# Constants and modulation columns inside the norm stage, output inputs in halves, and a last norm taken block by block

## The chip, the cores and the metric

The kernel runs as one program on 1 core of one Trainium2 chip. Its time is the device time in microseconds (us) of one execution; the time before is 3041.14 us, the median of 3 runs that lie between 3032.96 and 3041.2. TensorE multiplies matrices, VectorE and ScalarE work elementwise, GpSimd splits some of the weights, and SyncE issues most transfers (DMAs). In the profile these are PE (with PEld, its weight loads), DVE, ACT, POOL and SP; SPq and ACTq are transfers issued by SyncE and ScalarE.

## The reference

Two blocks over 1024 tokens of width 1024, one after the other, all in fp32. The change touches the seams of the second block:

```python
x = first_block(x, ...)                       # attention + state-space block, ends in rms_norm
mod   = silu(c) @ ada_w + ada_b               # 6 x 1024: shift, scale, gate of two norms
mod_c = silu(c_ctx) @ ada_w + ada_b
pc = modulate(rmsnorm(ctx, norm1_g), csh1, csc1) @ w_in     # 256 context tokens
px = modulate(rmsnorm(x, norm1_g), sh1, sc1) @ w_in         # 1024 tokens
# modulate(h, shift, scale) = h * (1 + scale) + shift
a_x = rwkv_out(rwkv_bidir(...)); b_x = short_conv(px_cv, conv_w)
x = x + g1 * (concatenate([a_x, b_x]) @ w_out)
hx = modulate(rmsnorm(x, norm2_g), sh2, sc2)
x = x + g2 * expert_choice_ffn(hx, router_w, w_gate, w_up, w_down)   # 16 experts
return rmsnorm(x, final_g)
# rmsnorm(x, g) = x * rsqrt(mean(x * x) + 1e-6) * g
```

## The kernel before, in words

The program is a sequence of stages. Each stage is a `Phase`, which holds its SBUF and PSUM tiles and semaphores; when it ends, the semaphores are cleared and a barrier over all engines follows (L85 to L90). Inside a stage every engine has an instruction stream of its own, written out by hand, and they meet only in semaphores. Tokens are taken in blocks of 128 (`P`), rows in `KD` = 8 parts of 128 columns. There is no planner: the order of everything is the order in the code.

**Constants of the second block** (`second_mixer`, L2637). A stage `const2` loads 24 tensors one after the other on SyncE's queue (`load_constants`, L103) and waits for all: two matrices of squares, an identity, twelve level masks of 32 KB, four triangular masks of 64 KB, the norm gain as columns (`n1`), three small tables for the projections, and last two rows of 2048 numbers, shift and scale for tokens and context (`rows`). Then a stage of its own (`affine_columns`, L1440) turns these rows into columns by 16 transposes on TensorE; VectorE adds 1 to the scale and multiplies by the gain: `ab`.

**Norm stage** (`mixer_norms`, L1462). Ten blocks: two of the context, eight of the first block's result `xmid`. SyncE loads into four buffers; from block 4 on each load waits until the block four before it is scaled (L1483). ScalarE squares with a running sum, VectorE makes the mean, ScalarE the root, VectorE the inverse, and scales the rows into `xn`. TensorE turns them by 8 transposes into PSUM; VectorE (columns 0 to 3) and ScalarE (4 to 7) apply `ab`. ScalarE rounds the result to its high part, VectorE subtracts for the low part. In each engine's stream block b's square or mean stands before block b-1's affine part.

**Projections, state recurrence, output.** The tables `mu`, `cls` and `taps` are used in `mixer_projections`, the masks and identity later. The last stage of the mixer is `out_norm` (L1106), named `o2` here; the first block ends in the same function under the name `on`, with other arguments (`late` empty, a norm in the end). For `o2` the left factor comes from memory in two parts of 2 MB, `aT` and `bT`, each [128, 4, 1024]; they are `late`, and SyncE asks for them first (L1131), then for the eight weight rows of 512 KB, into four buffers, so that weight 4 waits until weight 0 is split (L1134 to L1137). ScalarE and VectorE wait for both parts in full (L1175, L1206), split block 0 of the left factor (`put(0)`), then the weights, then block 1. TensorE does three matmuls for each weight row and half, eight blocks in all, and VectorE multiplies by the gate and adds `xmid`.

**Router and experts** follow, then `final_norm` (L3090): SyncE loads eight blocks and then the gain row, broadcast to all partitions; ScalarE squares all eight; one mean, one root, one inverse for all of them at once; then VectorE multiplies block by block into two buffers, each of which waits from block 2 on for the store of the block two before it (L3135).

Of the kernel before, what the change touches and what calls it, by code (L numbers as in the profile page):

```python
# [1105 lines left out]
def out_norm(nc, name, parts, late, w_dram, split, x_dram, gate, gain, y_dram):  # L1106
# [4 lines left out]
    with Phase(nc, name) as ph:  # L1111
# [9 lines left out]
        names = ("late", "row_loaded", "w_hi", "w_lo", "s_hi", "s_lo", "summed", "gated", "added", "squared", "meaned", "rooted", "inverted",  # L1121
# [6 lines left out]
        with nc.Block() as block:  # L1128
            @block.sync
            def _(sp):  # L1130
                for dst, src in late:  # L1131
                    sp.dma_start(dst, src).then_inc(q["late"], 16)
                for k in range(KD):
                    if k >= 4:  # L1134

                        sp.wait_ge(q["w_lo"], k - 3)
# [28 lines left out]
            def _(act):  # L1165
                def put(b):
                    if b >= 2:

                        act.wait_ge(q["summed"], b - 1)
# [5 lines left out]
                if late:  # L1175
                    act.wait_ge(q["late"], 16 * len(late))
# [20 lines left out]
            def _(dve):  # L1197
# [8 lines left out]
                if late:  # L1206
                    dve.wait_ge(q["late"], 16 * len(late))
# [232 lines left out]
def affine_columns(nc, T, rows, n1, ab):  # L1440

    with Phase(nc, "aff") as ph:
        pc = ph.ps("pc", [P, 2 * KD, 2])
        turned, made, scaled = ph.sem("turned"), ph.sem("made"), ph.sem("scaled")
        with nc.Block() as block:
            @block.tensor
            def _(pe):
                for k in range(2 * KD):
                    last = nc.tensor.transpose(pc[:, k, :], rows[:, k * P:(k + 1) * P], T.ident[0:2, 0:2])
                last.then_inc(turned, 1)  # L1450

            @block.vector
            def _(dve):
                dve.wait_ge(turned, 1)
                for row in range(2):
                    nc.vector.tensor_scalar(ab[:, 2 * row, :], pc[:, KD:, row], 1.0, None, ALU.add).then_inc(made, 1)
                    nc.vector.tensor_copy(ab[:, 2 * row + 1, :], pc[:, :KD, row]).then_inc(made, 1)
                    dve.wait_ge(made, 2 * row + 2)
                    nc.vector.tensor_tensor(ab[:, 2 * row, :], ab[:, 2 * row, :], n1, ALU.mult).then_inc(scaled, 1)


def mixer_norms(nc, T, blocks, parts):  # L1462
# [4 lines left out]
    with Phase(nc, "n2") as ph:  # L1467
# [3 lines left out]
        st = ph.sb("st", [P, 4, N])  # L1471
# [5 lines left out]
        with nc.Block() as block:  # L1477
            @block.sync
            def _(sp):
                for b in range(N):  # L1480
                    if b >= 4:

                        sp.wait_ge(q["normed"], b - 3)  # L1483
# [1802 lines left out]
```

## Time and profile before

| | us |
|---|---|
| median of 3 runs | 3041.14 |
| lowest, highest | 3032.96, 3041.2 |
| profiled execution | 3047.39 |
| its span, first to last instruction | 3045.5 |
| TensorE busy in it | 2514.2 (83%) |
| VectorE busy | 1639.6 (54%) |
| ScalarE busy | 987.2 (32%) |
| GpSimd busy | 631.3 (21%) |

The profile is of one execution. Times in its rows count from the start of the span. A row of the timeline gives the start, the duration, the engine, the line of the kernel, the operation with its output and inputs, how often it is merged into this row, and in brackets how long the engine stood idle before it and what released it. TensorE's granted clock has two levels, 1.2 and 2.4 GHz; the profile gives it as a share of the higher one. Tile names are the program's with digits left out: `b_aT` is `aT`, `n_xt` the norm stage's input buffer, `fin_y` the output buffer of the last norm.

### The profile page before, as it was taken

Reading aid. Unit: us, or ns where it says so; the run is one execution under the profiler, and the core shown is the slowest. Engines: PE = TensorE matmul, PEld = TensorE weight load, DVE = VectorE, ACT = ScalarE, POOL = GpSimd, SP = SyncE. Lnnn points to the kernel's source line nnn. Section 1 sums busy time; section 2 is a strip of 40 time slices with the busy share of each in tenths; the row PEclk is TensorE's granted clock in tenths of the full one; section 3 lists DMA queues with packets and bytes.
Section 4 is the critical chain, followed back from the end, with each engine's and each line's share of the span. In section 5 each row is a group of like instructions: output and inputs, shape, how many; then the busy total and the mean of one; then the engine's idle time right before and its main releaser. Section 6 shows DMA issues by size and latency. Waiting matters only on the chain. (4 is left out here: it accounts for less than half of the span.)

```text
span 3045.5 us, 57305 instructions
## 1 busy us (share of the span) xinstructions
PE 2514.2 (83%) x23846; PEld 1934.9 (64%) x23846; DVE 1639.6 (54%) x2057; ACT 987.2 (32%) x1546; POOL 631.3 (21%) x618
## 2 busy tenths in 40 slices
PE   4698997869989379997857888888763799999993
PEld 1586654546757368886336667774553788888882
DVE  2793447521114322565545556552336499999993
ACT  2111442210013320001324333332211087777772
POOL 0221357212210023220045444430000010110000
PEclk8899999989999679998569999995875599999996
DMA  9232004321113211110231011101533099999993
GB/s 381 70 135 79 10 1 133 100 96 52 34 56 124 94 49 63 49 42 18 102 93 31 18 25 30 26 4 56 190 119 138 20 391 403 398 388 398 399 380 132
DMA packets 132726, 405.60 MB, mean 133 GB/s; under 512 B 55090, under 2 KB 64946, under 8 KB 102690
## 3 DMA queue, kind: packets, MB, share of 16 engines
q1 hardware_dynamic: 119268, 359.53, 31.6%
q0 software_dynamic: 4608, 16.78, 2.3%
q10 hardware_dynamic: 8640, 26.19, 2.2%
q8 instruction: 169, 2.77, 0.4%
q14 instruction: 41, 0.34, 0.0%
HBM read 346.85 MB, written 55.61 MB: 132 GB/s over the span
## 5 line engine op out<-in xcount | busy, mean ns | idle before, releaser
L3039 DVE TENSOR_TENSOR ex_wl<-ew_raw,ex_wh 128x2048 fp32r<-128x2048 f32 x192 | 435.8, 2290 | 42.6 <-ACT ex_wh L3001 39.0
L3001 ACT ACTIVATE ex_wh<-ew_raw 128x2048 fp32r<-128x2048 f32 x192 | 367.6, 1919 | 216.8 <-PEq L89 109.3
L125 PE MATMUL sp_acc<-b2h_hi,sp_wh 128*128 128x512 f32 (+1 forms) x528 | 194.8, 369 | 11.7 <-POOL sp_wl L1614 11.7
L125 PE MATMUL sp_acc<-b2h_lo,sp_wh 128*128 128x512 f32 (+1 forms) x528 | 194.5, 368 | 0.0
L125 PE MATMUL sp_acc<-b2h_hi,sp_wl 128*128 128x512 f32 (+1 forms) x528 | 194.3, 368 | 0.0
L2162 ACT ACTIVATE rc_xt<-rc_ps 128x256 f32<-128x256 f32 x200 | 67.7, 389 | 197.2 <-PE rc_ps L2331 196.6
L2922 POOL DMA_INDIRECT x<-ex_o,ex_at x16 | 26.5, 1656 | 493.1 <-DVE ex_o L3062 493.1
L1100 DVE TENSOR_TENSOR merge_sg<-b_pj,merge_sg 128x512 f32<-128x512 f32 x16 | 11.1, 693 | 218.0 <-ACT merge_sg L1086 218.0
L2229 DVE TENSOR_TENSOR rc_x<-rc_x,rc_ps 128x256 f32<-128x256 f32 x160 | 60.2, 418 | 120.4 <-PE rc_ps L2317 120.1
L125 PE MATMUL merge_acc<-merge_hh,merge_wh 128*128 128x512 f32 x256 | 101.5, 396 | 26.4 <-POOL merge_wl L119 21.1
L125 PEld LDWEIGHTS sp_acc<-b2h_hi,sp_wh 128*128 128x128 f32 x528 | 100.1, 190 | 28.7 <-POOL sp_wl L1614 12.1
L1612 POOL CAST sp_wh<-sp_w 128x1024 fp32r<-128x1024 f32 x26 | 27.1, 1042 | 434.5 <-DMA sp_w<-in_w_conv 250.9
L2910 POOL DMA_INDIRECT ex_xs<-h,ex_at x16 | 26.7, 1667 | 422.1 <-DVE ex_at L3064 398.1
L125 PEld LDWEIGHTS sp_acc<-b2h_lo,sp_wh 128*128 128x128 f32 x528 | 100.2, 190 | 16.5
L125 PEld LDWEIGHTS sp_acc<-b2h_hi,sp_wl 128*128 128x128 f32 x528 | 100.0, 189 | 16.5
L125 PE MATMUL pr_acc<-h_hi,pr_wh 128*128 128x512 f32 x224 | 89.7, 400 | 21.8 <-POOL pr_wl L205 20.1
L2223 DVE TENSOR_TENSOR rc_t<-rc_ps,b_level 128x256 f32<-128x256 f32 x200 | 75.5, 419 | 52.7 <-PE rc_ps L2317 52.3
L2943 PE MATMUL ex_G<-ex_wh,ex_xh 128*128 128x512 f32 x256 | 102.3, 399 | 1.4 <-DVE ex_xl L3044 1.4
L2943 PE MATMUL ex_O<-ex_wh,ex_hh 128*128 128x512 f32 x256 | 100.4, 392 | 1.6 <-DVE ex_hl L3055 1.6
L2943 PE MATMUL ex_U<-ex_wh,ex_xh 128*128 128x512 f32 x256 | 101.1, 395 | 0.0
L2944 PE MATMUL ex_G<-ex_wl,ex_xh 128*128 128x512 f32 x256 | 100.8, 394 | 0.0
L2945 PE MATMUL ex_G<-ex_wh,ex_xl 128*128 128x512 f32 x256 | 100.7, 393 | 0.0
(465 smaller groups left out, 6364.6 us busy)
## 6 DMA issues: line engine op xcount, KB each, us to landing
ew_raw<-in_exp_gate SPq DMA_DIRECT2D x64, 1024.0 KB, 7.5
ew_raw<-in_exp_up SPq DMA_DIRECT2D x64, 1024.0 KB, 9.7
ew_raw<-in_exp_down SPq DMA_DIRECT2D x64, 1024.0 KB, 8.2
b_pj<-in_ada_w SPq DMA_DIRECT2D x24, 1024.0 KB, 19.1
rc_ac<-ac SPq DMA_DIRECT2D x40, 256.0 KB, 3.8
merge_w<-in_w_merge SPq DMA_DIRECT2D x16, 512.0 KB
ac<-rp_ac SPq DMA_DIRECT2D x4, 2048.0 KB, 7.2
pr_w<-in_w_main SPq DMA_DIRECT2D x14, 512.0 KB
```

The source lines that it names most:

```text
L125: ins = nc.tensor.matmul(out, w[a][:, k, :], h[b][:, k, cols], start=(first and n == 0), stop=(last and n == 2))
L1612: nc.gpsimd.tensor_copy(wh[:, i % 2], w[:]).then_inc(q["w_rounded"], 1)
L2162: A.activation(dst(t[d]), src(d), ACT.Copy, scale=scale).then_inc(q[d][ready], 1)
L2223: V.tensor_tensor(paired(b["t1"][:]), crossed(0, d), over(T.level[d][l + 1][:]), ALU.mult).then_inc(s["t1_ready"], 1)
L2229: V.tensor_tensor(paired(b["x"][:, sl]), paired(b["x"][:, sl]), crossed(0, d), ALU.subtract).then_inc(s["x_next"], 1)
L2910: nc.gpsimd.indirect_dma_start(xs[:, m % 2, :], None, h_dram, bass.IndirectOffsetOnAxis(at[:, m:m + 1], 0)).then_inc(gathered[m % 2], 16)
L2922: nc.gpsimd.indirect_dma_start(x2, bass.IndirectOffsetOnAxis(at[:, x:x + 1], 0), o[:, x % 2, :], None, compute_op=ALU.add).then_inc(scatte ...
L2943: nc.tensor.matmul(acc[:, c], ah[:, k, :], wh[:, s, kk, c], start=(k == 0), stop=False)
L2944: nc.tensor.matmul(acc[:, c], ah[:, k, :], wl[:, s, kk, c], start=False, stop=False)
L2945: last = nc.tensor.matmul(acc[:, c], al[:, k, :], wh[:, s, kk, c], start=False, stop=(k == KD - 1))
L3001: nc.scalar.activation(wh[:, n % RING], raw[:, n % RING], ACT.Copy).then_inc(q["w_hi"], 1)
L3039: V.tensor_tensor(wl[:, n % RING], raw[:, n % RING], wh[:, n % RING].bitcast(f32), ALU.subtract).then_inc(q["w_lo"], 1)
```

## The change

1. Stages `const2` and `affine_columns` are gone. The two rows and the gain are loaded at the head of the norm stage, before its first block; the transposes stand first in TensorE's stream of that stage, the six VectorE operations in iteration 1 of its loop, and ScalarE waits for `ab` before its affine part of block 0. The other 22 loads are issued between those of blocks 5 and 6, and SyncE waits for them at the end of the stage.
2. `out_norm` loads `aT` and `bT` in halves of 512 tokens. The first halves stand before weights 0 and 1 in the queue, both second halves before weight 4. ScalarE waits for the first halves before block 0 and for the second before block 4; VectorE's own wait is gone, since it waits for what ScalarE makes of them.
3. `final_norm` makes mean, root and inverse for each block, has one output buffer for each block, and loads the gain row after block 0.

```diff
@@ out_norm
-                for dst, src in late:
-                    sp.dma_start(dst, src).then_inc(q["late"], 16)
+                def late_half(i, h):
+                    dst, src = late[i]
+                    n = slice(h * (S // 2), (h + 1) * (S // 2))
+                    sp.dma_start(dst[:, :, n], src[:, :, n]).then_inc(q[f"late{h}"], 16)
+
                 for k in range(KD):
+                    if k < len(late):
+                        late_half(k, 0)
+                    if k == 4:
+                        for i in range(len(late)):
+                            late_half(i, 1)
                 def put(b):
+                    if late and b in (0, NB // 2):
+                        act.wait_ge(q["late1" if b else "late0"], 16 * len(late))
                     if b >= 2:
...
-                if late:
-                    act.wait_ge(q["late"], 16 * len(late))
...
-                if late:
-                    dve.wait_ge(q["late"], 16 * len(late))
                 put(0)
@@ affine_columns is gone; mixer_norms
-def mixer_norms(nc, T, blocks, parts):
+def mixer_norms(nc, T, blocks, parts, mod_rows, n1_row, ab, constants):
...
+                for dst, src in ((rows[:], mod_rows), (n1[:], n1_row)):
+                    sp.dma_start(dst, src).then_inc(q["rows_loaded"], 16)
                 for b in range(N):
+                    if b == 6:
+                        for dst, src in constants:
+                            sp.dma_start(dst, src).then_inc(q["constants_loaded"], 16)
                     if b >= 4:
 
                         sp.wait_ge(q["normed"], b - 3)
                     sp.dma_start(xt[:, b % 4, :], blocks[b][0]).then_inc(x_loaded[b % 4], 16)
+                sp.wait_ge(q["constants_loaded"], 16 * len(constants))
...
                 def affine(b):
+                    if b == 0:
+                        act.wait_ge(q["ab_ready"], 2)
                     act.wait_ge(q["transposed"], 2 * b + 2)
...
                 for b in range(N):
+                    if b == 1:
+                        dve.wait_ge(q["rows_turned"], 1)
+                        for row in range(2):
+                            V.tensor_scalar(ab[:, 2 * row, :], pc[:, KD:, row], 1.0, None, ALU.add).then_inc(q["ab_made"], 1)
+                            V.tensor_copy(ab[:, 2 * row + 1, :], pc[:, :KD, row]).then_inc(q["ab_made"], 1)
+                        dve.wait_ge(q["ab_made"], 4)
+                        for row in range(2):
+                            V.tensor_tensor(ab[:, 2 * row, :], ab[:, 2 * row, :], n1[:], ALU.mult).then_inc(q["ab_ready"], 1)
+                        dve.wait_ge(q["ab_ready"], 2)
                     dve.wait_ge(q["summed"], b + 1)
...
+                pe.wait_ge(q["rows_loaded"], 32)
+                for k in range(2 * KD):
+                    last = nc.tensor.transpose(pc[:, k, :], rows[:, k * P:(k + 1) * P], T.ident[0:2, 0:2])
+                last.then_inc(q["rows_turned"], 1)
@@ second_mixer
-        with Phase(nc, "b2m") as b2m:
-            rows = b2m.sb("rows", [2, 2 * D])
-            loads += [(n1[:], I["norm1_g"]), (mu[:], I["shift_mu"]), (cls[:], I["shift_classes"]), (taps[:], I["conv_taps"]), (rows[:], mod_dram[:, 0:2 * D])]
-            load_constants(nc, "const2", loads)
-            affine_columns(nc, T, rows[:], n1[:], ab)
+        loads += [(mu[:], I["shift_mu"]), (cls[:], I["shift_classes"]), (taps[:], I["conv_taps"])]
...
-                mixer_norms(nc, T, blocks, hT)
+                mixer_norms(nc, T, blocks, hT, mod_dram[:, 0:2 * D], I["norm1_g"], ab, loads)
@@ final_norm
-        y = ph.sb("y", [P, 2, D])
+        y = ph.sb("y", [P, NB, D])
...
+                    if b == 1:
+                        sp.dma_start(row[:], gain.to_broadcast([P, D])).then_inc(q["row_loaded"], 16)
                     sp.dma_start(x[:, b, :], x_dram[b * P:(b + 1) * P, :]).then_inc(x_loaded[b], 16)
-                sp.dma_start(row[:], gain.to_broadcast([P, D])).then_inc(q["row_loaded"], 16)
                 for b in range(NB):
                     sp.wait_ge(q["ready"], b + 1)
-                    sp.dma_start(out[b * P:(b + 1) * P, :], y[:, b % 2, :]).then_inc(q[f"stored{b % 2}"], 16)
-                for s in range(2):
-                    sp.wait_ge(q[f"stored{s}"], 16 * (NB // 2))
+                    sp.dma_start(out[b * P:(b + 1) * P, :], y[:, b, :]).then_inc(q["stored"], 16)
+                sp.wait_ge(q["stored"], 16 * NB)
 
             @block.scalar
             def _(act):
+                def root(b):
+                    act.wait_ge(q["meaned"], b + 1)
+                    nc.scalar.activation(st[:, 2, b:b + 1], st[:, 1, b:b + 1], ACT.Sqrt).then_inc(q["rooted"], 1)
+
                 for b in range(NB):
                     act.wait_ge(x_loaded[b], 16)
                     if b >= 2:
 
                         act.wait_ge(q["summed"], b - 1)
                     nc.scalar.activation(sq[:, b % 2, :], x[:, b, :], ACT.Square, accum_out=st[:, 0, b:b + 1]).then_inc(q["summed"], 1)
-                act.wait_ge(q["meaned"], 1)
-                nc.scalar.activation(st[:, 2, :], st[:, 1, :], ACT.Sqrt).then_inc(q["rooted"], 1)
+                    if b:
+                        root(b - 1)
+                root(NB - 1)
 
             @block.vector
             def _(dve):
                 V = nc.vector
-                dve.wait_ge(q["summed"], NB)
-                V.tensor_scalar(st[:, 1, :], st[:, 0, :], 1.0 / D, EPS, ALU.mult, ALU.add).then_inc(q["meaned"], 1)
-                dve.wait_ge(q["rooted"], 1)
-                V.reciprocal(st[:, 3, :], st[:, 2, :]).then_inc(q["inverted"], 1)
-                dve.wait_ge(q["inverted"], 1)
-                dve.wait_ge(q["row_loaded"], 16)
+
+                def mean(b):
+                    dve.wait_ge(q["summed"], b + 1)
+                    V.tensor_scalar(st[:, 1, b:b + 1], st[:, 0, b:b + 1], 1.0 / D, EPS, ALU.mult, ALU.add).then_inc(q["meaned"], 1)
+
+                mean(0)
                 for b in range(NB):
-                    if b >= 2:
-                        dve.wait_ge(q[f"stored{b % 2}"], 16 * (b // 2))
-                    V.scalar_tensor_tensor(y[:, b % 2, :], x[:, b, :], st[:, 3, b:b + 1], row[:], ALU.mult, ALU.mult).then_inc(q["ready"], 1)
+                    if b + 1 < NB:
+                        mean(b + 1)
+                    dve.wait_ge(q["rooted"], b + 1)
+                    V.reciprocal(st[:, 3, b:b + 1], st[:, 2, b:b + 1]).then_inc(q["inverted"], 1)
+                    if b == 0:
+                        dve.wait_ge(q["row_loaded"], 16)
+                    dve.wait_ge(q["inverted"], b + 1)
+                    V.scalar_tensor_tensor(y[:, b, :], x[:, b, :], st[:, 3, b:b + 1], row[:], ALU.mult, ALU.mult).then_inc(q["ready"], 1)
```

## Rows read from the trace of the kernel before

**Rows 1.** The page: span, and TensorE's granted clock (tenths) in 40 equal slices.
```profile
span 3045.5 us, 57305 instructions
...
PEclk8899999989999679998569999995875599999996
```

**Rows 2.** Timeline across the constants stage: start us, duration us, engine, line, operation, idle before.
```profile
1011.99 0.33 SPq L111 DMA_DIRECT2D b_ones_bd<-in_squares  x1
...
1023.01 0.29 SPq L111 DMA_DIRECT2D b2m_rows<-mod  x1
...
1025.89 1.84 PE L1449 MATMUL aff_pc<-all_ident,b2m_rows 2*128 2x2 f32 x16 [22.69 <-PEq L89]
1027.77 0.17 DVE L1456 TENSOR_SCALAR all_ab<-aff_pc 128x8 f32<-128x8 f32 x1 [19.45 <-PE aff_pc L1449]
...
1029.23 0.81 SPq L1484 DMA_DIRECT2D n_xt<-in_ctx  x2
...
1034.05 1.06 ACT L1506 ACTIVATE n_sq<-n_xt 128x1024 f32<-128x1024 f32 x1 [27.98 <-DMA n_xt<-in_ctx]
```

**Rows 3.** Timeline inside the second block's norm stage.
```profile
1037.82 1.37 DVE L1526 TENSOR_SCALAR n_val<-n_pt,all_ab 128x128 f32<-128x128 f32 x4 [0.97 <-PE n_pt L1560]
...
1040.50 0.75 DVE L1545 TENSOR_SCALAR n_xn<-n_xt,n_st 128x1024 f32<-128x1024 f32 x1
...
1059.81 1.04 ACT L1506 ACTIVATE n_sq<-n_xt 128x1024 f32<-128x1024 f32 x1
```

**Rows 4.** Timeline at the start of the second block's output stage.
```profile
2136.03 0.32 SPq L1132 DMA_DIRECT2D b_aT<-aT  x1
...
2149.03 0.63 ACT L1172 ACTIVATE o_sh<-b_aT 128x512 fp32r<-128x512 f32 x1 [35.06 <-DMA b_bT<-bx]
...
2152.77 0.76 PE L1159 MATMUL o_acc<-b_o_hi,o_sh 128*128 128x512 f32 x1 [20.48 <-DVE b_o_lo L1211]
...
2163.96 1.06 ACT L1180 ACTIVATE b_o_hi<-o_w 128x1024 fp32r<-128x1024 f32 x1 [0.91 <-DMA o_w<-in_w_out]
...
2166.33 0.50 PE L1159 MATMUL o_acc<-b_o_hi,o_sh 128*128 128x512 f32 x1 [0.33 <-DVE b_o_lo L1211]
```

**Rows 5.** Busy time by stretch: span, five engines, clock, DMA share, GB/s.
```profile
2139.00:2149.00 10.00, 0.00 (x0) 0.00 (x0) 0.00 (x0) 0.00 (x0) 0.00 (x0) 0.50 0.98 416
2984.00:2987.40 3.40, 2.77 (x7) 2.19 (x8) 0.57 (x1) 0.00 (x0) 0.00 (x0) 0.54 0.00 0
2987.40:2992.00 4.60, 4.60 (x21) 3.80 (x20) 0.00 (x0) 0.00 (x0) 0.00 (x0) 0.97 0.00 0
```

**Rows 6.** Stores in rows of 2 KB (L1759): issue to landing.
```profile
DMA to landing us min/median/max: 4.8/7.1/7.2
```

**Rows 7.** Timeline of the last norm.
```profile
3013.43 1.06 ACT L3120 ACTIVATE fin_sq<-fin_x 128x1024 f32<-128x1024 f32 x1 [29.69 <-DMA fin_x<-x]
...
3018.07 1.06 ACT L3120 ACTIVATE fin_sq<-fin_x 128x1024 f32<-128x1024 f32 x1 [1.43 <-DMA fin_x<-x]
...
3019.35 1.06 ACT L3120 ACTIVATE fin_sq<-fin_x 128x1024 f32<-128x1024 f32 x1
...
3025.61 1.28 ACT L3122 ACT_TABLE_LOAD   x1
...
3027.14 0.20 DVE L3130 RECIPROCAL fin_st<-fin_st 128x8 f32<-128x8 f32 x1 [1.35 <-ACT fin_st L3122]
3027.38 2.48 DVE L3136 SCALAR_TENSOR_TENSOR fin_y<-fin_x,fin_st,fin_row 128x1024 f32<-128x1024 f32 x2
...
3039.35 2.54 DVE L3136 SCALAR_TENSOR_TENSOR fin_y<-fin_x,fin_st,fin_row 128x1024 f32<-128x1024 f32 x2 [1.45 <-DMA out<-fin_y]
```

**Rows 8.** Chain of waits at the end: start us, us, what.
```profile
3028.70 2.66 DMA out<-fin_y
```

**Rows 9.** Timeline of the last block of the first output stage.
```profile
1004.50 1.06 ACT L1188 ACTIVATE on_sq<-on_y 128x1024 f32<-128x1024 f32 x1 [9.30 <-DVE on_y L1232]
...
1005.87 0.20 ACT L1190 ACTIVATE on_ss<-on_ss 128x1 f32<-128x1 f32 x1 [0.22 <-DVE on_ss L1234]
```

More of the change, by code:

```diff
@@ L1120, in out_norm @@
         acc = ph.ps("acc", [P, 2, 2, 512])
-        names = ("late", "row_loaded", "w_hi", "w_lo", "s_hi", "s_lo", "summed", "gated", "added", "squared", "meaned", "rooted", "inverted",
+        names = ("late0", "late1", "row_loaded", "w_hi", "w_lo", "s_hi", "s_lo", "summed", "gated", "added", "squared", "meaned", "rooted", "inverted",
                  "normed", "ready")
@@ L1437 @@
 DECAY = 0.6065306597126334
[L1440 to L1459, printed above, removed]
-def mixer_norms(nc, T, blocks, parts):
+def mixer_norms(nc, T, blocks, parts, mod_rows, n1_row, ab, constants):
     N = len(blocks)
@@ L1471, in mixer_norms @@
         st = ph.sb("st", [P, 4, N])
+        rows = ph.sb("rows", [2, 2 * D])
+        n1 = ph.sb("n1", [P, KD])
         val = ph.sb("val", [P, 2, KD, P])
         pt = ph.ps("pt", [P, 2, KD, P])
+        pc = ph.ps("pc", [P, 2 * KD, 2])
         x_loaded = [ph.sem(f"x_loaded{s}") for s in range(4)]
-        names = ("summed", "meaned", "rooted", "inverted", "normed", "transposed", "scaled", "shifted", "hi_done", "lo_done")
+        names = ("summed", "meaned", "rooted", "inverted", "normed", "transposed", "scaled", "shifted", "hi_done", "lo_done",
+                 "rows_loaded", "rows_turned", "ab_made", "ab_ready", "constants_loaded")
         q = {n: ph.sem(n) for n in names}
@@ L2649, in second_mixer @@
         loads += [(m[d][:], I["lower"][n, d]) for n, m in enumerate((T.minus, T.plus)) for d in range(2)]
-        n1 = b2.sb("n1", [P, KD])
         mu = b2.sb("mu", [P, RW_N])
@@ L3098, in final_norm @@
         x_loaded = [ph.sem(f"x_loaded{b}") for b in range(NB)]
-        names = ("row_loaded", "summed", "meaned", "rooted", "inverted", "scaled", "ready", "stored0", "stored1")
+        names = ("row_loaded", "summed", "meaned", "rooted", "inverted", "ready", "stored")
         q = {n: ph.sem(n) for n in names}
```

## The prediction

> **What bounds the kernel now.** The page comes first: its 40 slices say where TensorE's granted clock is full and where it is half [rows 1]. None of the three edited places is in a stretch where TensorE works at full clock; each is one in which most engines stand. So the question is not what an engine does but which wait ends last, and that is read from the timeline, stage by stage, then from the chain of waits at the end.
>
> Constants of the second block [rows 2]: the reader is to see SyncE issue from 1011.99 to 1023.01, the last being the two modulation rows, then sixteen small transposes at 1025.89, six small VectorE operations from 1027.77, and only at 1029.23 the first block of the norm stage, whose square starts at 1034.05. Nothing else runs: 17.24 us from the first constant to the issue of the first useful load.
>
> Output stage [rows 4]: loads are asked for from 2136.03, but ScalarE starts at 2149.03, when the last of 4.19 MB has landed; the engines move 416 GB/s meanwhile [rows 5]. TensorE starts at 2152.77 and then waits for weights; the eighth of them is rounded at 2163.96 and multiplied at 2166.33. DMA bytes bound this start.
>
> Last norm [rows 7]: ScalarE squares eight blocks, then one table load at 3025.61, then VectorE scales, in pairs of blocks, since two buffers make it wait 1.45 us before every later pair for a store that takes 2.66 us [rows 8].
>
> **Part 1: constants and columns inside the norm stage.** The first queue entries become the modulation rows (16 KB) and the norm gain (4 KB), then the first context block. The 24 issues from 1011.99 to 1023.01 are 23 steps in 11.02 us, 0.48 us each [rows 2]; the first issue itself takes 0.33. Two issues ahead of the context block put it at 1011.99 + 0.37 + 0.47 = 1012.83 (the gaps by these two durations), against 1029.23: 16.4 us earlier. Landing then took 4.82 us to the square; the two small transfers ahead may add up to 0.5. I take a gain of 16.2, bounds 15.5 and 16.6.
>
> What must be hidden for this. The transposes (1.84 us) need rows that before were used 2.88 us after their issue, a barrier included [rows 2]; now 1012.4 + 2.9 + 1.9 = 1017.2, while the first square is at 1017.8. TensorE's first block transposes are later still. The six VectorE operations come between scaling block 0 and the mean of block 1. At 0.17 us each, unoverlapped, they cost 1.0 us; VectorE stood 0.97 us at this point waiting for TensorE [rows 3]. Cover equals cost; without cover it would be 1 us once. ScalarE's wait for the columns stands before its half of the same block, behind which its root of block 1 and all later squares queue; the columns are ready before TensorE's transposes are, so nothing is late.
>
> The other 22 constants (two squares, identity, twelve levels, four masks, three small ones) are now issued between the loads of blocks 5 and 6. Block 5's load waits for the scaling of block 1, which began at 1040.50 and took 0.75 [rows 3]. In old time: constants 1041.3 + 0.4 to 1041.7 + 22 x 0.48 = 1052.3, then block 6, landing with the 4.82 us of rows 2 at 1057.1. Its square was due at 1059.81 [rows 3]: 2.7 us of slack. Blocks 7 to 9 are issued right behind and are due one step apart; a step is (1059.81 - 1041.25) / 4 = 4.64 us, since the square of block 6 starts as the scaling of block 5 ends. SyncE's closing wait for the constants is met long before the stage ends. So: nothing; the other end, if small rows drain at half the issue rate, is 10.6 us more, of which 2.7 are covered: 7.9 lost.
>
> **Part 2: output inputs in halves.** New queue order: aT first half (1.05 MB), weight 0, x 0, bT first half, weight 1, x 1, weights 2 and 3, then both second halves, then weights 4 to 7. ScalarE and VectorE can start when 3.15 MB are there and not 4.19: 1.05 MB / 416 GB/s = 2.5 us earlier, at 2146.5. The end of this start is set by weight 7. All before it is 4.19 + 4.19 + 1.05 = 9.44 MB whichever way it is ordered; after 2149.03 a queue without holes needs 5.24 MB / 416 = 12.6 us, so weight 7 lands at 2161.6, against 2163.96 now, because weights 4 to 7 wait for a free buffer while the queue runs dry. The new order frees buffers earlier (the first at about 2150.2) while second halves still fill the queue to 2156.6, so no hole arises. Gain up to 2.3. The rows now become 2 KB long where they were 16 KB; stores in 2 KB rows landed 2 MB in 7.1 us [rows 6], and 2.10 MB / 416 is 5.0, leaving 2.1 for the fixed part, so such rows cost at most some 4% of 4.19 MB, 0.4 us.
>
> TensorE: weight 4 lands three steps of 1.26 us (0.52 MB / 416) before weight 7, at 2157.8, and like that one is multiplied 2.37 us later [rows 4], at 2160.2. The 24 matmuls of weights 0 to 3, begun at 2150.3, take 0.43 us at half clock and 0.22 at full [rows 5]; with half of them at each they end at 2158.1: an idle stretch of 2.1 us. In the last expert, where a gap of 4.0 us held only 1.09 us of transposes, the clock was 0.54 for 3.4 us and 7 matmuls, while 21 took 4.60 us after it [rows 5]: 0.40 to 0.49 each instead of 0.22, 1.5 us lost. Mine is half as long; I take the value without a fall, 1.8 us, with 0.3 as the other end.
>
> The Trainium skill, "DMA: Bandwidth & Descriptors", section "Measured", gives 6.15 us (341 GB/s) for a 1 MB transfer and asks for at least that size. By an estimate from that rate the 3.15 MB would take 9.2 us, not 7.6, and part 2 would gain next to nothing; the trace disagrees for a full queue, 416 GB/s [rows 5].
>
> **Part 3: last norm block by block.** x 0 lands as before (square at 3013.43). The gain row, 0.52 MB, now goes before x 1, so each later block lands one step later: the square of block 1 at 3018.07, where block 2's was, instead of two blocks by then [rows 7]. It ends 1.2 us later; the table load (1.28) follows at 3019.3, the root of block 0 at 3020.5, its inverse, and the first product at 3021.0, against 3027.38. From there VectorE has, for each block, a product (2.48 for two, so 1.20 apart), a mean of 0.06 (overlapped) and an inverse with 0.24 to the product [rows 7]: 1.50 to 1.72 us if nothing overlaps. ScalarE needs 1.28 for a square (3018.07 to 3019.35) and 0.20 for a root [rows 9], 1.48. Take 1.55: the eighth product starts 3021.0 + 10.85 = 3031.85 and ends 3033.1. Before, the last ended 3039.35 + 2.54 = 3041.89. With the same last store behind both: gain 8.8; 7.6 at 1.72 us. Eight output buffers take away the 1.45 us waits. Stores come 0.52 MB every 1.55 us, 338 GB/s, under the 416. The first stores queue behind the last x loads, but nobody waits for them. I take 8.5, bounds 7 and 10 (a row that costs the loads nothing gives the upper one).
>
> **Sum.** 16.2 + 1.8 + 8.5 = 26.5 us. The profiled execution took 3047.39 (span 3045.5), 6.25 above the median 3041.14; 3047.39 - 26.5 = 3020.9, and the same saving from the median gives 3014.6 us, my figure.
>
> **Rivals.**
> A. The halves gain nothing: 1.8 falls to 0.3 or below, because the clock falls in the new gap [rows 5] or 2 KB loads are slower than 2 KB stores. Time 3016.1. Against it: the gap is short; for it: the same kind of gap was seen once. 0.17.
> B. Constants hold block 6: SyncE and queue serve 22 small transfers just when the stage wants 0.52 MB every 4.64 us. 7.9 us lost, 3022.5. Against: before, the last of them was used 2.88 us after its issue [rows 2], so the queue keeps up with the issue. 0.07.
> C. The last norm alternates Square and Sqrt on ScalarE, and each turn reloads a table: 12 more loads of 1.28 us [rows 7], 15.4 us, which makes that part a loss of 6.9 and the time 3030.0. Against: in the first output stage a square at 1004.50 is followed by a root at 1005.87 with VectorE's mean between and no load [rows 9]. 0.02. The Trainium skill, "ScalarE: Activation LUTs", section "Table sets: the hidden batching unit", says to do all functions of one set before the next; it prices a switch at 2.66 us, by which this estimate would be 32 us.
> D. Slower than before: the second block's projections, right after the norm stage, run under another granted clock. The page shows the slices from 990 to 1142 us (the 14th and 15th, 76 us each) at 6 and 7 tenths and the next three at 9 [rows 1]. A full-clock matmul takes 0.22 us, one at half clock about 0.43 [rows 5]; the 26.5 us are gone from 126 such matmuls on, some 54 us at half clock. Against: TensorE there has no gaps and the change touches none of it. 0.02, 3045 or more.
> E. The idle stretch was not only the constants': something else (the stores of the first block's result, semaphore clearing) holds the norm stage's first load. Each microsecond of it comes off the 16.2; at half, 3022.7. 0.04.
>
> **How the numbers follow.** Forecast 0.68, A 0.17, B 0.07, E 0.04, C 0.02, D 0.02. The parts' bounds sum to 22.8 and 28.9 us; the three runs shown spread from 3032.96 to 3041.20, so a median may sit some 4 us lower. That gives 3007 to 3018 for the forecast; with A, B and half of E up to 3023. No change means within 0.3%, 9.1 us, about what a measurement of this kernel tells: only C or a large E comes there. Faster 0.95, same 0.03, slower 0.02.
>
> **What would show it.** Norm stage: first context load 0.84 us behind the first issue of the stage, its blocks still 4.64 us apart, no idle time before block 6's square put down to its load. Output stage: first ScalarE copy near 10.5 us after the first issue instead of 13.0, weight 7 rounded 2.3 us earlier relative to it, and the clock column at 1.00 after the warm-up. Last norm: a single table load, products 1.5 to 1.7 us apart, none waiting for a store, the last one 19 to 20 us after x 0's square instead of 28.5 with its duration. I am wrong if the first square of the norm stage comes less than 15 us earlier, or if the last norm gains under 7.

## The result, and the profile after

| | before | changed |
|---|---|---|
| median of 4 runs, us | 3038.91 | 3003.61 |
| lowest, highest | 3032.96, 3041.2 | 3000.45, 3011.73 |
| profiled execution, us (span) | 3047.39 (3045.5) | 3006.41 (3004.3) |

The ratio is 0.9891, with a 95% interval from 0.9864 to 0.9918: faster by some 33 us. 26.5 us and 3014.6 were forecast, with a range down to 3007.0, so the median lies 3.4 us under the range. In the page, span and TensorE's clock by slices:

```profile
span 3004.3 us, 57281 instructions
...
PEclk8899999979999789998579999996875599999997
```

Where the time of the two profiled executions went, by places that both traces have (us; a stage is read from one engine's start to the next stage's):

| stretch | before | changed | difference |
|---|---|---|---|
| start to last store of the first block's result | 1008.3 | 1007.7 | -0.6 |
| to the first square of the norm stage (part 1) | 25.7 | 8.2 | -17.5 |
| norm stage, projections, preparation | 533.6 | 534.6 | +0.9 |
| state recurrence, first to last matmul | 487.1 | 475.9 | -11.1 |
| to the first load of the output stage | 81.2 | 78.5 | -2.7 |
| output stage, to the router's first load (part 2) | 118.6 | 120.7 | +2.1 |
| router and experts, to the last norm's first load | 755.3 | 753.0 | -2.3 |
| last norm, first load to last store issued (part 3) | 32.0 | 21.6 | -10.4 |
| from there to the end of the span | 3.6 | 4.1 | +0.5 |

Three of these are stages that the change edits; with the end of the last of them, in the last row, they come to 25.3 us. The other 15.8 us fell where nothing was edited; whether they belong to the change is what the experiments had to tell.

**Norm stage** [rows 2, 3]. Timeline of the changed kernel:

```profile
1007.70 0.33 ACTq L1200 DMA_DIRECT2D xmid<-on_y  x1
1011.34 0.26 SPq L1469 DMA_DIRECT2D n_rows<-mod  x1
...
1012.04 0.90 SPq L1477 DMA_DIRECT2D n_xt<-in_ctx  x2
...
1013.60 1.87 PE L1560 MATMUL n_pc<-all_ident,n_rows 2*128 2x2 f32 x16 [11.04 <-DMA n_n<-in_norm_g]
1015.95 1.06 ACT L1502 ACTIVATE n_sq<-n_xt 128x1024 f32<-128x1024 f32 x1 [10.52 <-DMA n_xt<-in_ctx]
...
1018.42 0.16 DVE L1534 TENSOR_SCALAR all_ab<-n_pc 128x8 f32<-128x8 f32 x1
...
1019.11 0.15 DVE L1541 TENSOR_SCALAR n_st<-n_st 128x1 f32<-128x1 f32 x1
1019.72 1.36 DVE L1522 TENSOR_SCALAR n_val<-n_pt,all_ab 128x128 f32<-128x128 f32 x4 [0.46 <-PE n_pt L1569]
...
1034.28 7.84 SPq L1477 DMA_DIRECT2D n_xt<-xmid  x4
```

The first context block is asked for 0.70 us after the stage's first transfer and squared 3.91 us later, not 4.82. The transposes run at 1013.60, in time that ScalarE waits anyway. The columns take VectorE from 1018.42 to the mean of block 1 at 1019.11, 0.7 us, and it still waits 0.46 for TensorE (0.97 in rows 3). Block 6 is asked for at 1034.28, after the 22 constants, and no later square of the stage waits for a load.

**Output stage** [rows 4, 5]. Timeline, then busy time by stretch:

```profile
2104.93 0.55 SPq L1134 DMA_DIRECT2D b_aT<-aT  x1
...
2115.75 0.63 ACT L1182 ACTIVATE o_sh<-b_aT 128x512 fp32r<-128x512 f32 x1 [32.89 <-DMA b_bT<-bx]
...
2119.13 4.67 SPq L1145 DMA_DIRECT2D o_w<-in_w_out  x4
...
2119.25 0.77 PE L1167 MATMUL o_acc<-b_o_hi,o_sh 128*128 128x512 f32 x1 [18.07 <-DVE b_o_lo L1217]
...
2128.92 1.06 ACT L1188 ACTIVATE b_o_hi<-o_w 128x1024 fp32r<-128x1024 f32 x1 [6.72 <-DMA o_w<-in_w_out]
...
2131.29 0.79 PE L1167 MATMUL o_acc<-b_o_hi,o_sh 128*128 128x512 f32 x1 [4.32 <-DVE b_o_lo L1217]
...
2132.74 1.06 ACT L1188 ACTIVATE b_o_hi<-o_w 128x1024 fp32r<-128x1024 f32 x1 [0.19 <-DMA o_w<-in_w_out]
```

```profile
2119.00:2125.00 6.00, 5.75 (x17) 4.61 (x17) 3.69 (x4) 2.11 (x2) 0.00 (x0) 0.62 1.04 391
2125.00:2130.00 5.00, 1.97 (x9) 1.31 (x7) 0.00 (x0) 1.06 (x1) 0.00 (x0) 1.00 1.04 410
2130.00:2132.00 2.00, 0.71 (x2) 0.62 (x3) 1.93 (x2) 1.57 (x2) 0.00 (x0) 0.60 0.83 330
2132.00:2137.00 5.00, 5.00 (x14) 3.84 (x12) 4.18 (x5) 2.65 (x4) 0.00 (x0) 0.50 0.02 9
2137.00:2140.00 3.00, 3.00 (x14) 2.51 (x13) 0.11 (x1) 0.17 (x1) 0.00 (x0) 0.96 0.00 0
```

ScalarE starts 10.8 us after the first issue (13.0 before). But weight 4, asked for 14.2 us after it, is rounded only 24.0 us after it, behind an idle time of 6.72 us; weight 7 27.8 us after it (27.9 before). TensorE stands 4.32 us, and its clock falls before it starts again: 0.60 in the stretch from 2130, then 0.50. By their rows 12 matmuls start in the 5 us from 2132, and 12 in the 3 us from 2137 (the 14 in each stretch above include two that began before it). The gain at the head is given back.

**Last norm** [rows 7 to 9]:

```profile
2978.63 0.33 SPq L3111 DMA_DIRECT2D fin_x<-x  x1
...
2982.03 1.06 ACT L3128 ACTIVATE fin_sq<-fin_x 128x1024 f32<-128x1024 f32 x1 [27.60 <-DMA fin_x<-x]
...
2985.80 1.06 ACT L3128 ACTIVATE fin_sq<-fin_x 128x1024 f32<-128x1024 f32 x1 [2.62 <-DMA fin_x<-x]
...
2986.96 1.28 ACT L3121 ACT_TABLE_LOAD   x1
...
2988.77 1.29 DVE L3150 SCALAR_TENSOR_TENSOR fin_y<-fin_x,fin_st,fin_row 128x1024 f32<-128x1024 f32 x1
...
2990.22 1.28 DVE L3150 SCALAR_TENSOR_TENSOR fin_y<-fin_x,fin_st,fin_row 128x1024 f32<-128x1024 f32 x1
...
2998.89 1.28 DVE L3150 SCALAR_TENSOR_TENSOR fin_y<-fin_x,fin_st,fin_row 128x1024 f32<-128x1024 f32 x1
```

One table load, as forecast; it stands ahead of the first product, since ScalarE reaches it only after the square of block 1. Products are 1.45 us apart and none waits for a store. But the stage ends only when the stores have landed. Issues of the stores, then busy time by stretch:

```profile
2990.08 10.45 SPq L3114 DMA_DIRECT2D out<-fin_y  x8
```

```profile
2984.00:2988.00 4.00, 0.00 (x0) 0.00 (x0) 0.15 (x1) 2.19 (x3) 0.00 (x0) 0.50 1.02 418
...
3000.00:3002.00 2.00, 0.00 (x0) 0.00 (x0) 0.17 (x1) 0.00 (x0) 0.00 (x0) 0.50 1.01 414
3002.00:3004.30 2.30, 0.00 (x0) 0.00 (x0) 0.00 (x0) 0.00 (x0) 0.00 (x0) 0.50 0.26 107
```

From 2984 to 3002 the DMA engines move 414 to 422 GB/s without a pause, first loads and then stores; the stage's 17 transfers of 0.52 MB are 8.9 MB. VectorE's last product ends at 3000.17, the span at 3004.3. So it is the queue, and no engine, that ends this stage; e8 below tests it.

### The profile page after: what moved, and what is told of

Same layout as the page of the kernel before. It is cut to its first block and busy times, and to the rows that moved or that the text cites. A ratio compares the mean times of both kernels' runs of the same rounds, so it can differ in the third digit from the quotient of the medians.

```text
span 3004.3 us, 57281 instructions
## 1 busy us (share of the span) xinstructions
PE 2508.3 (83%) x23846; PEld 1929.6 (64%) x23846; DVE 1639.2 (55%) x2071; ACT 986.5 (33%) x1553; POOL 627.4 (21%) x618
## 5 line engine op out<-in xcount | busy, mean ns | idle before, releaser
L2926 POOL DMA_INDIRECT x<-ex_o,ex_at x16 | 26.5, 1655 | 495.2 <-DVE ex_o L3066 463.9
L1100 DVE TENSOR_TENSOR merge_sg<-b_pj,merge_sg 128x512 f32<-128x512 f32 x16 | 11.1, 692 | 217.6 <-ACT merge_sg L1086 217.6
L125 PE MATMUL merge_acc<-merge_hh,merge_wh 128*128 128x512 f32 x256 | 101.5, 396 | 25.9 <-POOL merge_wl L119 20.5
L125 PE MATMUL merge_acc<-merge_hl,merge_wh 128*128 128x512 f32 x256 | 100.6, 393 | 0.0
L125 PE MATMUL merge_acc<-merge_hh,merge_wl 128*128 128x512 f32 x256 | 100.4, 392 | 0.0
## 6 DMA issues: line engine op xcount, KB each, us to landing
b_pj<-in_ada_w SPq DMA_DIRECT2D x24, 1024.0 KB, 18.6
```

The source lines that it names most:

```text
L125: ins = nc.tensor.matmul(out, w[a][:, k, :], h[b][:, k, cols], start=(first and n == 0), stop=(last and n == 2))
L1100: nc.vector.tensor_tensor(sg[:, h, 0:1, :], merged[:, ds(b, 1), h * 512:(h + 1) * 512], sg[:, h, 0:1, :], ALU.mult).then_inc(weighed, 1)
L2926: nc.gpsimd.indirect_dma_start(x2, bass.IndirectOffsetOnAxis(at[:, x:x + 1], 0), o[:, x % 2, :], None, compute_op=ALU.add).then_inc(scatte ...
```

## The experiments

Theory L: each part acts in its own stage alone, and the rest is what differs from one execution to the next. Theory S: something in part 1 also shortens the state recurrence. Ratios are to the kernel before, timed beside it; "output stage" and "last norm" are read as in the table, the last norm to the issue of its last store.

**Each part alone.** The edits are those of the change's own diff, one part at a time; e4 leaves out part 2.

```diff
 e1: only affine_columns / mixer_norms / second_mixer of the diff
 e2: only out_norm
 e3: only final_norm
 e4: all but out_norm
```

> The kernel before with part 1 alone (constants and columns inside the norm stage). Theory L (each part acts only in its own stage; the rest of the fall is clock and loop timing that differs from run to run): first square 17.4 us earlier against the last store of the first block, so 0.9943 of the time before; the state recurrence (first to last of its TensorE work, 487 us before, 476 in the changed kernel) may come out at either. Theory S (part 1 also makes the state recurrence faster, by the shifted start or by the 32 bytes that the tiles behind the gain columns moved): 17.4 + 11 + 3 = 31 us, 0.990, with a recurrence near 476 us.

> The kernel before with part 2 alone (output inputs in halves). Theory L: a loss of 2.9 us as in the changed kernel's profile: ScalarE starts some 2.2 us earlier, but weight 4 lands no earlier against the first issue of the stage, TensorE idles over 4 us before it and restarts at a granted clock of 0.5: ratio 1.001, 1.0000 to 1.0015. Rival (the fall of the clock was a chance of that one execution): a gain of up to 0.3 us, since the landing of weight 7 moves by 0.1 only; the prediction's own figure was a gain of 1.8 (0.9994).

> The kernel before with part 3 alone (last norm block by block). Theory L: from the first load's issue to the last product 31.99 us before, 21.5 now: a gain of 10 us, 0.9967. The prediction's figure was 8.5. Theory S says the same of this run; the state recurrence should be at 487 us by it, since nothing ahead of the last norm has changed.

> Parts 1 and 3 without part 2. Theory L: 17.4 + 10.0 = 27.4 us, ratio 0.9910, which is faster than the changed kernel's own parts (24.5 us) by the 2.9 us that the halves lose. Theory S: 38 to 41 us, ratio 0.987, with a recurrence near 476 us.

| | ratio, interval | us of 3042 | recurrence | output stage | last norm |
|---|---|---|---|---|---|
| e1 | 0.9942 (0.9926 to 0.9957) | -17.6 | 482.8 | 117.0 | 30.9 |
| e2 | 1.0014 (1.0002 to 1.0026) | +4.3 | 486.2 | 119.6 | 31.0 |
| e3 | 0.9964 (0.9952 to 0.9975) | -11.0 | 485.5 | 118.0 | 21.5 |
| e4 | 0.9903 (0.9887 to 0.9920) | -29.5 | 477.3 | 117.7 | 21.4 |

Theory L's four figures (0.9943, 1.001, 0.9967, 0.9910) are met; S's 0.990 for e1 and 0.987 for e4 are excluded, though e4's recurrence came out near the 476 us that S names. Part 2 is a loss. The parts add up to 24.3 us, but the intervals of the three reach 3.5 to 4.7 us to either side, so by my estimate the sum is known to some 7 us only.

**The whole again, and what the halves do.**

```diff
 e6, SyncE's stream of out_norm
-                    if k == 4:
-                        for i in range(len(late)):
-                            late_half(i, 1)
...
                 sp.dma_start(row[:], ...)
+                for i in range(len(late)):
+                    late_half(i, 1)
 e7, ahead of all weights; block 0 waits for late0 and late1
+                    if k == 0:
+                        for h in range(2):
+                            for i in range(len(late)):
+                                late_half(i, h)
```

> The changed kernel itself, to narrow its interval (0.9864 to 0.9918). Theory L (the parts alone: 17.6 + 11.0 - 4.3 = 24.3 us by the runs of each): ratio 0.9920. Theory S (something beyond the parts, as the 33 us of the first measurement suggest): 0.9891. In its profile the state recurrence is below 480 us by S and anywhere between 476 and 487 by L.

> The changed kernel, but both second halves are asked for behind weight 7 and the gate row instead of before weight 4. Theory G (part 2 loses because 2.1 MB that nobody needs yet stand in the queue before weight 4, TensorE idles over 4 us and its granted clock falls): weight 4 is rounded some 18 to 19 us after the first issue of the stage (24.0 in the changed kernel), weight 7 near 22.5 (27.8), no second fall of the clock, block 2 of the left factor written near 26.5 us (34.9): 8 us less than the changed kernel, 5 less than the old order, ratio to before 0.989 to 0.990. Rival R (the halves lose because rows of 2 KB move slower, whatever the order): weight 7 would still come 24 us or later, and the ratio stays within 2 us of that of the changed kernel in this call.

> The changed kernel, but all four halves stand at the head of the queue and block 0 waits for all of them: the order of the kernel before with rows of 2 KB in place of 16 KB. Theory G: the rows cost little; ScalarE starts 13.4 to 14 us after the first issue (13.0 before), no idle stretch of TensorE over 1 us once it has begun, one rise of the clock only, the stage ends within 1 us of the old one and 3 us ahead of the changed kernel. Rival R: ScalarE starts 15 us or later and the stage is as long as in the changed kernel.

Measured: e5 0.9907 (0.9890 to 0.9923), e6 0.9880 (0.9859 to 0.9900), e7 0.9890 (0.9871 to 0.9910). Output stage 120.1, 113.6 and 118.8 us. Timeline of e6:

```profile
2106.97 0.55 SPq L1134 DMA_DIRECT2D b_aT<-aT  x1
...
2124.75 1.06 ACT L1187 ACTIVATE b_o_hi<-o_w 128x1024 fp32r<-128x1024 f32 x1 [0.91 <-DMA o_w<-in_w_out]
...
2130.73 1.06 ACT L1187 ACTIVATE b_o_hi<-o_w 128x1024 fp32r<-128x1024 f32 x1 [1.17 <-DMA o_w<-in_w_out]
...
2133.10 0.50 PE L1166 MATMUL o_acc<-b_o_hi,o_sh 128*128 128x512 f32 x1 [0.45 <-DVE b_o_lo L1216]
```

```profile
2125.00:2130.00 5.00, 5.00 (x23) 3.91 (x22) 2.96 (x4) 2.93 (x3) 0.00 (x0) 1.00 0.88 297
2130.00:2135.00 5.00, 4.55 (x20) 3.42 (x19) 3.39 (x5) 2.31 (x4) 0.00 (x0) 1.00 1.01 379
```

Weight 4 is rounded 17.8 us after the first issue (18 to 19 expected), weight 7 at 23.8 (22.5 expected), and once it has begun TensorE never waits more than 0.45 us. The output stage is 6.5 us shorter than e5's (8 expected) and 4.3 shorter than the mean of the six profiles in the old order, 117.9 (5 expected). Weight 7 alone would not have told G from R, which said 24 us or later; the stage's length, the clock that stays at 1.00 and a median 10.8 us under e5's do. Theory G is right, and R is wrong as the whole of the cause. Timeline of e7:

```profile
2111.23 0.55 SPq L1134 DMA_DIRECT2D b_aT<-aT  x1
...
2124.95 0.63 ACT L1182 ACTIVATE o_sh<-b_aT 128x512 fp32r<-128x512 f32 x1 [35.80 <-DMA b_bT<-bx]
...
2140.14 1.06 ACT L1188 ACTIVATE b_o_hi<-o_w 128x1024 fp32r<-128x1024 f32 x1 [1.71 <-DMA o_w<-in_w_out]
...
2142.51 0.50 PE L1166 MATMUL o_acc<-b_o_hi,o_sh 128*128 128x512 f32 x1 [0.93 <-DVE b_o_lo L1217]
```

With the old order and rows of 2 KB, ScalarE starts 13.7 us after the first issue (13.0 before, 12.5 to 12.7 in the other five profiles of that order) and weight 7 is rounded at 28.9 (27.9): the short rows, with four requests in place of two, cost about 1 us of a 4.19 MB load. TensorE stands 0.93 us at most and its clock does not fall again. The stage is 0.8 us longer than the 117.9 of the old order, and 1.4 us shorter than e5's, where theory G had said 3: R's short rows have a share.

All profiles agree on the rest. In the eight with the order of the changed kernel (after, e2, e5, e8, e10, e11, e14, e16) TensorE stands 3.1 to 4.8 us before weight 4 and its clock then falls to 0.50 for some 3 to 7 us; in the other ten it stands 1.4 us at most and the clock, once up, stays. The stage takes 120.2 us on average in the eight and 117.9 in the six with the old order and long rows: 2.2 us lost, of which e7, a single profile, gives some 0.8 to the short rows. The rest is the order's, with the idle stretch and the clock behind it.

**The last norm's table load and gain row.**

```diff
 e8, ScalarE's stream of final_norm
-                    if b:
-                        root(b - 1)
+                    if b != 1:
+                        root(max(b - 1, 0))
 e9 = e6 + e8, and in SyncE's stream
-                    if b == 1:
+                    if b == 2:
                         sp.dma_start(row[:], ...)
```

> The changed kernel, but in the last norm the root of block 0 stands before the square of block 1, so the table load falls into ScalarE's wait for block 1 (2.6 us). If the table load is on the path, the second product starts earlier; the first product, at 10.1 us after the first load's issue in the changed kernel, comes near 7 us (then it waits for the gain row), the last one 1.3 to 2 us earlier than its 20.3. If VectorE's own pace binds from the second block on, the gain is as large, since its chain starts with the second product; if the landing of blocks binds, the gain is nil.

> The changed kernel with the second halves behind the weights, the root of block 0 ahead of the square of block 1, and the gain row behind x block 1. By the stages' own times: output stage 1.9 us shorter than before (6.5 shorter than in the changed kernel: 98.9 to 92.4), last norm 19.9 - 1.3 = 18.6 us from first issue to last store (32.0 before, 21.3 in the changed kernel), norm stage 17.5 us: 17.5 + 1.9 + 13.4 = 32.8 us, ratio 0.9892. If the row behind block 1 only moves the wait from ScalarE to VectorE, the last norm stays at 19.9 and the ratio is 0.9896.

e8 0.9903 (0.9887 to 0.9920), e9 0.9900 (0.9880 to 0.9921). Last norm 19.9 us in e8, 21.4 in e9, against 21.5 in the changed kernel. Timelines of e8 and then e9:

```profile
2983.02 0.33 SPq L3111 DMA_DIRECT2D fin_x<-x  x1
...
2987.65 1.28 ACT L3121 ACT_TABLE_LOAD   x1
...
2989.93 1.06 ACT L3128 ACTIVATE fin_sq<-fin_x 128x1024 f32<-128x1024 f32 x1 [0.78 <-DMA fin_x<-x]
...
2991.44 1.29 DVE L3150 SCALAR_TENSOR_TENSOR fin_y<-fin_x,fin_st,fin_row 128x1024 f32<-128x1024 f32 x1
...
2992.90 1.28 DVE L3150 SCALAR_TENSOR_TENSOR fin_y<-fin_x,fin_st,fin_row 128x1024 f32<-128x1024 f32 x1
```

```profile
2986.51 1.28 DVE L3149 SCALAR_TENSOR_TENSOR fin_y<-fin_x,fin_st,fin_row 128x1024 f32<-128x1024 f32 x1 [1.38 <-DMA fin_row<-in_final_g]
...
2987.82 1.06 ACT L3127 ACTIVATE fin_sq<-fin_x 128x1024 f32<-128x1024 f32 x1 [2.95 <-DMA fin_x<-x]
...
2989.30 1.28 DVE L3149 SCALAR_TENSOR_TENSOR fin_y<-fin_x,fin_st,fin_row 128x1024 f32<-128x1024 f32 x1
```

In e8 the table load sits in ScalarE's wait, and the first product is 8.4 us after the first load's issue instead of 10.1, the last store is issued 1.6 us earlier. It is not 7 us: VectorE's mean of block 1 stands before the inverse of block 0. In e9 the row behind block 1 makes the first product wait 1.38 us for it and block 2's square wait 2.95: the gain of e8 is lost again. The figure of 18.6 us that I had expected was wrong.

But even e8's gain is none at the end of the program. Busy time by stretch at its end:

```profile
3004.00:3006.00 2.00, 0.00 (x0) 0.00 (x0) 0.00 (x0) 0.00 (x0) 0.00 (x0) 0.50 1.03 422
3006.00:3008.70 2.70, 0.00 (x0) 0.00 (x0) 0.00 (x0) 0.00 (x0) 0.00 (x0) 0.50 0.28 114
```

The last product ends at 3002.84 and the queue goes on at 422 GB/s for over 3 us. From the first load's issue to the end of the span the last norm takes 25.6 us in e8, against 25.7, 25.9, 26.2 and 26.2 in the four profiles of the changed kernel and 27.0 in e9. Stores that are issued earlier only wait longer in the queue: of its three outcomes, the expectation's last one (the landing of blocks binds, the gain is nil) is nearest, with the stores' landing in the place of the loads'.

**Is there anything beyond the parts?** Only the tile addresses changed:

```diff
 e11, e14: changed kernel      e12: kernel before
+        b2.sb("n1pad", [P, KD])
         mu = b2.sb("mu", [P, RW_N])
-        n1 = b2.sb("n1", [P, KD])
+            n1 = b2m.sb("n1", [P, KD])
```

> The changed kernel with an unused tile of 32 bytes a partition where the gain columns stood, so that every later tile of the second block has its old address. Theory A (the 32 bytes by which those tiles moved make the state recurrence some 4 to 6 us shorter): the recurrence comes at 485 to 487 us, and the ratio near 0.9920, the parts alone. Theory L (nothing beyond the parts; the recurrence differs from execution to execution): 476 to 485 us, mean 480 as in the nine kernels with part 1.

> The kernel before with the gain columns in the short-lived scope of the modulation rows, and nothing else changed: the later tiles of the second block move by 32 bytes, to the addresses that they have in the changed kernel. Theory A: recurrence near 480 us, ratio 0.998 to 0.9985. Theory L: ratio 1.000 within 0.0015, recurrence anywhere from 476 to 487.

> The changed kernel a third time, beside the best one. Theory L: ratio 0.992, 24 us, as the parts alone; the two measurements so far gave 0.9891 and 0.9907. Theory S: 0.989 again. What decides whether the parts explain the whole is the mean of the three: below 0.990 something acts beyond them; at 0.9905 or above the difference to 0.9920 is no larger than their intervals.

> The changed kernel beside it. Parts alone 0.9920; mean of the measurements so far (with the one at old addresses) 0.9899. If this one is again at or below 0.991, some 3 to 5 us of the whole are not in the parts' own stages.

e11 0.9885 (0.9871 to 0.9899), recurrence 482.9 and in its second profile (e14) 480.8; e12 0.9997 (0.9987 to 1.0007), 483.2; the kernel before once more, for its profile alone (e13), 486.1. The addresses are not it: the fall stays with the old ones and does not come with the new ones alone. e10 0.9911 (0.9885 to 0.9938), e16 0.9924 (0.9900 to 0.9949). Busy time over the whole recurrence, first in the changed kernel's first profile, then in e16, the same program:

```profile
1550.50:2026.40 475.90, 392.80 (x13948) 337.89 (x13948) 266.84 (x646) 179.84 (x580) 219.03 (x337) 0.98 0.10 23
```

```profile
1551.30:2038.60 487.30, 397.51 (x13944) 341.91 (x13948) 267.15 (x646) 179.94 (x580) 219.06 (x337) 0.97 0.10 22
```

11.4 us between two executions of one program, with the same instructions (four matmul records of some 13,900 are missing from the second) and a mean clock of 0.98 against 0.97. Four measurements of the changed kernel give 0.9891, 0.9907, 0.9911 and 0.9924, mean 0.9908; the parts alone, added up (24.3 of 3042 us), give 0.9920, inside the intervals of the last three and 0.0002 above that of the first. These timings alone do not show anything beyond the parts. e11 does not fit, though: it is the changed kernel but for an unused tile, and its interval ends below 0.9920.

The profiles tell more than the timings. The recurrence took 475.9 to 485.4 us in twelve profiles with part 1 and 487.3 in one, mean 481.2; it took 483.2 to 487.1 in five without it, mean 485.6. In 59 of the 65 pairs of one and the other, the one with part 1 is the shorter. And it matches the times: by the stages' own lengths, read to the end of the span, part 1 gives 17.1 us, part 2 takes 2.2 and part 3 gives 8.9 (means over the profiles with and without each), 23.7 in all for the changed kernel; the twelve timings of kernels with part 1 lie on average 4.4 us beyond such sums (from 0.6 below to 11.3 above), the three without it (e2, e3, e12) 0.3. So a recurrence some 4 us shorter goes with part 1, as theory S has it, though at less than half the size that S took; e1 alone (17.6, interval 13.1 to 22.5) allows it as well as its absence. Why is open. The addresses are ruled out, and half-clock time explains only some of it (e10's recurrence is among the shorter at 479.6 with a clock of 0.97).

**The best version.** The changed kernel with the edits of e6 and e8:

> The changed kernel with the second halves behind the weights and the root of block 0 ahead of the square of block 1; the gain row stays behind x block 0. By the stages: output stage 113.5 us from its first issue to the router's first load (117.8 in the old order, 120.3 in the changed kernel), last norm 19.9 us from its first load's issue to its last store's (31.3 before, 21.5 in the changed kernel), norm stage 17.5: 17.5 + 4.3 + 11.6 = 33.4 us, ratio 0.989, and 8.4 us (0.28%) under the changed kernel of this call. With the 5 us or so that whole kernels gained beyond their parts: 0.9875.

0.9902 (0.9879 to 0.9925), median 3011.74, beside e16's 3021.33: 9.6 us less, 8.4 expected. Output stage 113.4 us, last norm 19.8 to its last store's issue. But to the end of the span the last norm takes 26.1 us against e16's 26.2, so the mended stages are worth 7.5 and 0.2 us, and that 9.6 lies near the expected 8.4 is in part luck: in the two profiles e16's recurrence alone is 5.1 us longer. Against the kernel before the ratio missed the expected 0.989 by 0.0012, inside its interval; the other figure, 0.9875, lies just outside.

## Why the prediction was right or wrong

**Part 1 was right in its mechanism** and a little too small, outside its own bounds of 15.5 to 16.6: 16.2 forecast, 17.5 read in the two profiles, 17.1 as the mean over all, 17.6 timed in e1. The excess is the first block's load, 3.91 us against the 4.82 that I took and something for the small transfers ahead. That 4.82 was one draw: in the five profiles without part 1 this load took 3.55 to 5.05 us, in those with it 3.74 to 4.09. The covers held as named: columns, transposes and the 22 constants cost nothing (first to tenth square 39.7 us in both profiles), and rivals B and E did not occur; nor did D.

**Part 2 was wrong, in sign.** The step that failed: "so no hole arises. Gain up to 2.3", and behind it "an idle stretch of 2.1 us ... I take the value without a fall". The queue has no hole, but I let it move 416 GB/s throughout, while with short rows and more issues 7.2 MB had gone 20 us after the first issue (and 7.2 in e7), where the kernel before had moved 7.6. Weight 4 was rounded at 24.0 us, 2.2 later than worked out; the stretch became 4.3 us and the clock fell, as rows 5 had shown for a gap of 4.0. The 0.4 us "at most" for rows of 2 KB rested on a fixed part of 2.1 us that was only what was left over, and no row gave it; e7 showed 0.7 to 1.2 us. Rival A had the mechanism and too small a price: not 1.5 us less gain, but 2.2 us longer than the old order by the stage (120.2 against 117.9), 4.3 by e2's timing, whose interval is 0.6 to 7.9. More important, I worked out the order only against what lands first, not against what is needed next: the second halves, due for block 4 some 40 us later, stood before weight 4, due at once. e6 shows that by itself.

**Part 3 came out near its figure, with a wrong step in it.** 8.5 forecast; to the issue of the last store 10.4 in the two profiles and 9.5 against the 31.0 us of e1 and e2; to the end of the span 8.9 (34.7 us on average in the five profiles with the old norm, 25.9 in the ten with the new one); 11.0 timed in e3 (7.6 to 14.6). The pace was 1.45 us a product, not 1.55, as mean and inverse overlap. The step that failed is "The first stores queue behind the last x loads, but nobody waits for them", with "the same last store behind both": loads and stores are 8.9 MB at 414 to 422 GB/s, and the last store waits for all of them. Before, 3.6 us passed from its issue to the end of the span; in the changed kernel 4.1 to 4.7, in e8 5.8. The quicker pace and the later landing nearly cancel, which is luck. Rival C (table reloads) did not occur: one load, as rows 9 implied. It took 1.28 us; the 2.66 us that the Trainium skill, "ScalarE: Activation LUTs", states for a switch stand in its section "What ACT_TABLE_LOAD costs", and here the root of block 0 starts right behind the load (2988.26 after 2986.96 and 1.28), so nothing is seen of the rest.

**The sum was near, in part by luck**: 26.5 forecast; 23.7 by the stages' own lengths, 24.3 timed part by part, 28 as the mean of four measurements of the whole. Part 1 gave about 1 more, part 2 about 4 less, and some 4 us came in a recurrence that the prediction put at nothing.

**The range was wrong.** The failed step is "a median may sit some 4 us lower". Medians of the one program in four measurements were 3003.61, 3015.75, 3009.98 and 3021.33: the first lies below 3007, the last above the forecast's own 3018 and near the 3023 of the rivals, and their mean, 3012.7, is 1.9 us from the forecast. Three of them are known to come from three different chips; the kernel before, timed beside them, stayed between 3037.69 and 3042.24. I took the spread of three runs for that of a median, and did not look for a stage whose length can differ by 11 us with the same instructions. (The lower end is also mis-added: 3041.14 - 28.9 - 4 is 3008.2, not 3007.) In the profile of the first result the edited stages gave 25.3 us, near the forecast, and the recurrence, at 475.9 us the shortest of all eighteen, 11.1 more. That is what put the result outside the range, as far as one profile tells; how much of it is part 1's and how much chance stays open.

## What to carry to other kernels

When a transfer is cut so that work can start on its first part, put the rest behind everything that is due sooner, and work out the landing of the next thing needed, not of the first. A stall that is shortened at its head can come back as a gap that costs TensorE its clock. When a stage ends in stores, read its length to their landing and not to their issue: where the queue is full to the end, a faster engine gains nothing. Judge single microseconds by the stage's own length and by each part alone; medians of the whole moved by 17.7 us here, more than any part was worth. And when the whole gains more than its parts, compare the untouched stages over many profiles before calling it noise.

## What the runs showed of the hardware

A load of 4.19 MB in rows of 2 KB and four requests took about 1 us longer to its first use than in rows of 16 KB and two requests (13.7 us in e7, against 12.5 to 13.0 in six profiles).

TensorE's granted clock fell from 2.4 to 1.2 GHz in each of the eight profiles in which it stood 3.1 to 4.8 us before weight 4, and in none of the ten in which it stood 1.4 us or less. In the changed kernel's first profile the idle stretch was 4.3 us; 12 matmuls started in the 5 us from 2132, at half clock, and 12 in the 3 us after that. In e6 no wait of TensorE for weight 4 or a later one was above 0.45 us, and its clock stood at 1.00 from 2125 to 2140.

In the last norm of the changed kernel the DMA engines moved 414 to 422 GB/s for 18 us, loads and then stores of 0.52 MB queued behind each other; with all stores issued 1.6 us earlier (e8) the stage ended 25.6 us after its first load's issue, against 25.7 to 26.2.

Square and Sqrt alternated on ScalarE over eight blocks with one table load of 1.28 us.
